# One narrow VectorE instruction of differential attention, written as SCALAR_TENSOR_TENSOR in place of TENSOR_SCALAR

## The reference

```python
def diff_attn_core(q, k, v, lam):
    s = jnp.einsum('bhiqd,bhikd->bhiqk', q, k).astype(jnp.float32) * (q.shape[-1] ** -0.5)
    p = jax.nn.softmax(s, axis=-1)
    a = (p[:, :, 0] - lam * p[:, :, 1]).astype(v.dtype)
    return jnp.einsum('bhqk,bhkd->bhqd', a, v)
```

## Time and profile before

| | |
|---|---|
| time, median of 3 runs | 1615.28 us (1615.06 to 1615.35) |
| the profiled execution's own time | 1616.29 us |
| its span in the trace | 1614.5 us |
| mean granted TensorE clock | 0.996 |
| TensorE busy | 1593.2 us, 99% of the span |
| VectorE busy | 983.0 us, 61% |
| ScalarE busy | 518.3 us, 32% |
| GpSimd busy | 617.7 us, 38% |
| attention loop of layer 1 | from about 1084 to 1188 us of the span |

### The profile page before, as it was taken

One profiled execution on the slowest core, in us unless ns is written; L12 is line 12 of the kernel. 1 busy time (PEld: TensorE's weight loads), 2 busy tenths in 40 slices (PEclk: granted clock), 3 DMA queues, 4 the chain that ended last, 5 costly groups with the idle time before them and its releaser, 6 DMA issues.

```text
span 1614.5 us, 24201 instructions
## 1 busy us (share of the span) xinstructions
PE 1593.2 (99%) x9427; PEld 1431.8 (89%) x9427; DVE 983.0 (61%) x1314; ACT 518.3 (32%) x933; POOL 617.7 (38%) x402
## 2 busy tenths in 40 slices
PE   8999999999999999999999999999999999999997
PEld 5889988989999999999999888878889888888887
DVE  4697457258756764864784678229975825344354
ACT  4422466333211211211211512138864422222222
POOL 2422565335323322432331544244505644444441
PEclk9999999999999999999999999999999999999998
DMA  9473212213252234233332122110002322223221
GB/s 359 183 284 134 92 41 99 91 67 105 74 188 78 79 120 141 96 99 117 105 112 98 66 92 92 65 56 1 1 1 92 105 92 94 102 92 104 91 79 53
DMA packets 50334, 162.99 MB, mean 101 GB/s; under 512 B 6336, under 2 KB 8768, under 8 KB 46656
## 3 DMA queue, kind: packets, MB, share of 16 engines
q1 hardware_dynamic: 50240, 161.68, 28.9%
HBM read 158.78 MB, written 2.10 MB: 100 GB/s over the span
## 4 chain that ended last, share of the span: by engine, by line
PE 92%; DVE 3%; DMA 2%; issue 1%; ACT 1%; SPq 0%; POOL 0%; POOLq 0%; DVEq 0%; ACTq 0%
PE ps L1706 26%; PE ps L1707 26%; PE ps L1708 26%; PE ps L2232 3%; PE ps L2194 2%; PE ps L2221 1%; PE ps L2099 1%; PE ps L2087 1%; PE ps L2127 1%; PE ps L1911 1%; DMA mod_late<-w_mod_dram 1%; DMA mod_big<-w_mod_dram 1%; DVE h L1311 1%; PE ps L2122 1%; DVE tmp_a L1302 1%
## 5 line engine op out<-in xcount | busy, mean ns | idle before, releaser
L621 POOL TENSOR_TENSOR w_lo<-raw,w_hi 128x1024 fp32r<-128x1024 f32 (+1 forms) x235 | 483.2, 2069 | 838.1 <-ACT w_hi L780 837.9
L1706 PE MATMUL ps<-h,w_hi 128*128 128x384 f32 (+2 forms) x1176 | 409.8, 348 | 1.7 <-DVE h L1311 1.2
L1707 PE MATMUL ps<-h,w_lo 128*128 128x384 f32 (+2 forms) x1176 | 407.6, 347 | 0.0
L1708 PE MATMUL ps<-h,w_hi 128*128 128x384 f32 (+2 forms) x1176 | 407.2, 346 | 0.0
L780 ACT ACTIVATE w_hi<-raw 128x1024 fp32r<-128x1024 f32 x187 | 197.8, 1058 | 371.5 <-PE ps L1708 365.7
L1706 PE MATMUL ps<-hid_lo,w_hi 128*128 128x384 f32 (+2 forms) x800 | 277.6, 347 | 0.0
L1707 PE MATMUL ps<-hid_hi,w_lo 128*128 128x384 f32 (+2 forms) x800 | 276.5, 346 | 0.0
L1708 PE MATMUL ps<-hid_hi,w_hi 128*128 128x384 f32 (+2 forms) x800 | 276.4, 346 | 0.0
L1706 PEld LDWEIGHTS ps<-h,w_hi 128*128 128x128 f32 x1176 | 221.3, 188 | 25.2 <-issue 3.4
L1708 PEld LDWEIGHTS ps<-h,w_hi 128*128 128x128 f32 x1176 | 221.2, 188 | 16.3
L1707 PEld LDWEIGHTS ps<-h,w_lo 128*128 128x128 f32 x1176 | 221.4, 188 | 16.0
(11 more groups left out here) (232 smaller groups left out, 2264.7 us busy)
## 6 DMA issues: line engine op xcount, KB each, us to landing
raw<-units_dram SPq DMA_DIRECT2D x187, 512.0 KB, 3.3
mod_ring<-w_mod_dram SPq DMA_DIRECT2D x96, 256.0 KB, 3.4
mod_big<-w_mod_dram SPq DMA_DIRECT2D x16, 1024.0 KB, 10.4
mod_late<-w_mod_dram SPq DMA_DIRECT2D x8, 1024.0 KB, 7.8
xl<-x_dram SPq DMA_DIRECT2D x2, 2048.0 KB, 8.4
bias<-bias_dram SPq DMA_DIRECT2D x8, 384.0 KB, 3.6
xc<-ctx_dram SPq DMA_DIRECT2D x2, 1024.0 KB, 10.5
out_dram<-out_t SPq DMA_DIRECT2D x16, 128.0 KB, 1.9
```

Source lines behind the costliest of these rows:

```text
L621: ins = nc.gpsimd.tensor_tensor(w_lo[:, s, sl], raw[:, s, sl], w_hi[:, s, sl].bitcast(F32), op=ALU.subtract)
L1706: mm(out, a[0], b[1], start=start, stop=False)
L1707: mm(out, a[1], b[0], start=False, stop=False)
L1708: return mm(out, a[0], b[0], start=False, stop=stop)
```

## The change

The product of the reciprocal with two per-partition values was a TENSOR_SCALAR with two scalars read from memory. It becomes a SCALAR_TENSOR_TENSOR: one scalar from memory (`lam_t[:, 4:5]`), and the row sum `l_first[:, n:n + 1]` as a second tensor input. Shapes (128x1), tiles and the order of the multiplications are the same; nothing else in the program is changed.

```diff
                 st.wait(V.reciprocal(stat[:, d:d + 1], stat[:, c:c + 1]))
-                st.wait(V.tensor_scalar(stat[:, d + 1:d + 2], stat[:, d:d + 1], lam_t[:, 4:5], l_first[:, n:n + 1],
-                                        ALU.mult, ALU.mult))
+                st.wait(V.scalar_tensor_tensor(out=stat[:, d + 1:d + 2], in0=stat[:, d:d + 1], scalar=lam_t[:, 4:5],
+                                               in1=l_first[:, n:n + 1], op0=ALU.mult, op1=ALU.mult))
```

## The result

| | before | after |
|---|---|---|
| median | 1616.26 us (17 runs, 1615.06 to 1618.69) | 1619.88 us (17 runs, 1617.95 to 1622.50) |
| ratio | 1 | 1.0022, 95% interval 1.0016 to 1.0029 |
| span of the profiled execution | 1614.5 us | 1616.8 us |
| attention loop, first reciprocal to last | 102.50 us | 105.88 us |

The change makes the kernel slower by about 3.6 us. 2.6 was forecast, and the median lies above the range, whose upper end was 1619.3. (The median of before is now over 17 runs, so it differs from that of the first three.)

A forecast was written before the change was run, and what follows sets the result against it. TensorE with ScalarE's exponentials behind it was taken as the bound. 0.6 us at the loop's start plus 4 x 0.5 = 2.0 us gave 2.6 us on 1615.28, so 1617.9 us, range 1615.1 to 1619.3.

The forecast's parts named there:

- The bound, and VectorE nearly on the path once per head: Attention loop: TensorE with ScalarE's exponentials behind it sets a 3.35 us beat; VectorE comes within 0.1 us slack once per head.
- The instruction's own price, 0.205 us: Narrow instruction at L1641, unblocked: 148 + 55 ns, 0.07 us less than the old form; ends 0.148 and 0.273.
- The double wait: Narrow instruction waits for GpSimd's whole current instruction, then L1646 for its next; L1646 takes about 1.8 us twice per group.
- One head, 0.5 us, four times: Turns 11 to 13 and later heads: blocking makes TensorE's scores 0.5 us later; four of five groups pay, 2.0 us.
- The loop's start, 0.6 us: Turn 2: narrow instruction and L1646 both blocked by GpSimd, 0.7 us later less 0.1 slack, costing 0.6 us.
- In turns 0 and 1 I count no gain: Loop's start: turn 0's reductions wait for scores and turn 1's L1646 for a GpSimd cast anyway, so nothing counted.
- The sum: Whole kernel: 0.6 us at the loop's start plus 2.0 us in four later heads, 2.6 us more, 0.16%.
- (c): Rival, loop: first of five groups costs too, no slack, narrow instruction 0.27; 4.2 us more, to 1619.5; chance 0.17.
- The range: Whole kernel's median: 1615.1 to 1619.3 us, leaving out the faster rival, half the no-blocking rival and the top of (c).
- The signs named ahead: Loop trace: narrow median near 0.205 us, maximum 0.6 to 0.9; L1646 about 1.8 twice per group; four 3.85 us score steps.

## Why the prediction was wrong, point by point

- **The bound, and VectorE nearly on the path once per head.** Right. The steps of the scores stretch only after blocked turns and at the low clock.
- **The instruction's own price, 0.205 us.** Measured about 0.22 when unblocked, inside the ends given. The gain of 0.05 us in a turn is worth about 0.1 us in the loop, and the forecast counted it at nothing.
- **The double wait.** Right in mechanism and place for the later heads, and shown from both sides: it is gone with one tensor input, and gone with short GpSimd instructions. The sentence taken from the Trainium skill (page "SBUF — State Buffer", section "Who interferes with whom") on instructions with at most one SBUF input leaves out that section's condition, that the instruction is outside the 2-port performance modes. In which mode the old form runs no run shows; that it is free of GpSimd here rests on the 272 to 276 ns of all 32.
- **One head, 0.5 us, four times.** Measured 0.45 us, four times, in the four heads named, the first group free. Turn 13 was to start 7.91 us after the scores of turn 11 and started after 8.00 (1128.48 - 1120.48); from turn 12 to 13 it is 3.91 us in both.
- **The loop's start, 0.6 us. This is the step that failed.** The sentence "In turns 0 and 1 I count no gain", with L1646 waiting "for a GpSimd cast anyway", put turn 1 at nothing. In the trace of before the narrow instruction of turn 1 starts at 1087.37 and the cast at 1087.44, and the prediction did not ask what the shortened turn 0 does to those 0.07 us. At full clock the start costs 2.93 - 1.8 = 1.1 us: 0.5 on VectorE in turn 1 and 0.8 in turn 2 (0.7 was forecast), less slack. In turn 2 the size was near, but the instructions were others than those walked through: GpSimd was ahead by then, and the two waits were for its first and second L735 (from 1090.33, 1.41 us together).
- **The clock was left out, the other part of the same failure.** No term and no rival had it. The wait in front of the transposition of turn 1 grew from 1.3 to 1.9 us, and in three of the four profiles with such a wait and nothing to fill it the clock fell, for 0.45 to 1.5 us more. The trace of before held the wait but no fall, so its price could have been bounded only from rows at the low clock elsewhere.
- **The sum.** 2.0 + 0.6 = 2.6 forecast; 1.8 + 1.1 + (0.45 to 1.5) = 3.4 to 4.4 in the profiles, 3.6 in the medians. The forecast is 0.7 of what was measured. The rival (c), "more than forecast", named about the right size with the wrong parts: the first of the five groups stayed free.
- **The range** went to 1619.3, just under (c) at 1619.5, and stood on a median of three runs that was 1.0 us below that of 17. The level was 1.0 us too low and the sum 1.0 us too small; with either one right the median would have lain inside.
- **The signs named ahead.** The narrow instruction's median is near the one given and its maximum inside the range given (0.222 and 0.848 us). L1646 does not take 1.8 us twice in a group: it takes 1.53 and 1.45, since the narrow instruction, at 0.55 and 0.59, sits out part of the wait. In place of one step of 3.85 there are two, 3.52 and 3.63.

## What to carry to other kernels

Before giving a small VectorE instruction a second SBUF tensor as input, look at what GpSimd does in the same turn: the small one waits for GpSimd's whole instruction, and the next large one then waits for the one after. A TENSOR_SCALAR with two scalars from memory costs 0.05 us more and is free of this. And when an edit moves one engine by hundredths of a microsecond, list the rows where two engines start within 0.1 us of each other, since those change hands; and ask of each wait on TensorE that grows whether the clock will hold. Nor should a level come from three runs: the first three of the kernel before were all among the five fastest of its 17.

## What the runs showed of the hardware

- An instruction with two SBUF tensors of one element per partition is blocked as one of 768 is: 0.85 us for 0.22. It ends 0.02 to 0.03 us after GpSimd's instruction. With two scalars from memory and one tensor all 32 took 0.27 us, and with one scalar and one tensor all 32 took 0.21. An input in PSUM did not count in the case shown: a 128x512 with one input there and one in SBUF took its usual 0.69 us inside a GpSimd instruction, the next one with both in SBUF 1.38.
- Who is first is not decided by the start in the trace alone: the narrow instruction 0.01 or 0.02 us ahead of GpSimd's still waited, and 0.07 ahead it did not.
- In all three profiles with both turns blocked and nothing in the waits, a wait of 1.86 to 1.88 us on TensorE was followed by a fall of the granted clock from 2.4 to 1.2 GHz, about 0.5, 1.1 and 0.9 us after the wait's end and each time ahead of turn 2's narrow instruction. With turn 1 alone blocked the wait was as long (1.87) and the clock held, in the one profile taken. As the three falls came before turn 2 was blocked, that blocking does not explain them; why the one profile held stays open. In the runs with the new form in turns 0 to 2 both cases seem to occur: four have a mean granted clock of 0.997 or 0.998 and took 1616.5 to 1618.3 us, seven have 0.994 or 0.995 and took 1619.0 to 1620.8. In the nine other profiles, where no single wait of the loop's start was above 1.34 us, the clock held.
